# A ring of 7 and 9 staging buffers for the expert weights, in place of 4

## The reference, cut to what matters

```python
def ec_moe(x, w_router, w_gate, w_up, w_down):
    cap = EC_CAPACITY * t // N_EXPERTS
    aff = jax.nn.softmax(jnp.einsum('btd,de->bet', x, w_router), axis=1)
    gate, idx = lax.top_k(aff, cap)
    xs = jax.vmap(lambda xb, ib: xb[ib])(x, idx)
    hid = silu(einsum('becd,edf->becf', xs, w_gate)) * einsum('becd,edf->becf', xs, w_up)
    y = einsum('becf,efd->becd', hid, w_down) * gate[..., None]
    return jax.vmap(lambda yb, ib: jnp.zeros((t, d), yb.dtype).at[ib].add(yb))(y, idx)
```

## Time and profile before

| what | value |
| --- | --- |
| median of three runs | 1483.58 us (1479.49 to 1487.28) |
| the profiled execution: its own time | 1485.16 us |
| its span, first to last instruction | 1483.4 us |
| PE, DVE, ACT, POOL busy | 86%, 60%, 50%, 15% of the span |
| mean rate of all DMA | 218 GB/s (323.19 MB) |
| experts of layer 0, first row transpose to last matmul | 396.9 to 712.6 us |
| experts of layer 1, first row transpose | 1138.65 us |

### The profile page before, as it was taken

One profiled execution on the slowest core, in us unless ns is written; L12 is line 12 of the kernel. 1 busy time (PEld: TensorE's weight loads), 2 busy tenths in 40 slices (PEclk: granted clock), 3 DMA queues, 4 the chain that ended last, 5 costly groups with the idle time before them and its releaser, 6 DMA issues.

```text
span 1483.4 us, 18079 instructions
## 1 busy us (share of the span) xinstructions
PE 1275.2 (86%) x7500; PEld 919.3 (62%) x7500; DVE 886.8 (60%) x997; ACT 736.8 (50%) x866; POOL 218.8 (15%) x128
## 2 busy tenths in 40 slices
PE   5799988997499899999559999999976998999991
PEld 3796856893365555655149994667934655656550
DVE  3613456326688777787164452553257888888883
ACT  3531056415377676776144214453155666666662
POOL 3000000020112121211150000000202023333130
PEclk9897899999699999999779999799997999999996
DMA  9710180004899999999873222002049999999985
GB/s 346 223 61 29 58 298 31 1 29 174 280 324 361 352 355 358 351 366 355 294 211 97 76 61 98 1 1 86 29 170 315 333 351 347 354 347 354 359 311 169
DMA packets 99047, 323.19 MB, mean 218 GB/s; under 512 B 6367, under 2 KB 30142, under 8 KB 82582
## 3 DMA queue, kind: packets, MB, share of 16 engines
q1 hardware_dynamic: 87360, 283.54, 53.3%
q0 software_dynamic: 9152, 30.53, 8.0%
q10 hardware_dynamic: 2454, 7.96, 1.3%
HBM read 298.20 MB, written 23.81 MB: 217 GB/s over the span
## 4 chain that ended last, share of the span: by engine, by line
PE 48%; DMA 21%; ACT 13%; DVE 13%; issue 3%; POOL 1%; ACTq 0%; SPq 0%; POOLq 0%; DVEq 0%
PE psum L821 45%; DVE w_lo L1774 8%; DMA stage<-in_moe_w_up 6%; DMA stage<-in_moe_w_gate 5%; ACT w_hi L1676 5%; DMA stage<-in_moe_w_down 4%; ACT arena L1601 3%; DMA stage<-in_w_mod 2%; DVE arena L2050 2%; DMA h_dram<-arena 1%; DMA acc_dram<-arena 1%; ACT arena L1374 1%; POOL arena L706 1%; DVE h_lo L1774 1%; ACT arena L1423 1%
## 5 line engine op out<-in xcount | busy, mean ns | idle before, releaser
L1774 DVE TENSOR_TENSOR w_lo<-stage,w_hi 128x2048 fp32r<-128x2048 f32 (+1 forms) x216 | 490.7, 2280 | 192.7 <-ACT w_hi L1676 120.7
L1676 ACT ACTIVATE w_hi<-stage 128x2048 fp32r<-128x2048 f32 x192 | 366.6, 1913 | 153.4 <-DMA stage<-in_moe_w_gate 43.0
L821 PE MATMUL psum<-w_hi,h_hi 128*80 128x512 f32 (+1 forms) x848 | 332.4, 392 | 51.8 <-DVE w_lo L1774 40.8
L821 PE MATMUL psum<-w_lo,h_hi 128*80 128x512 f32 (+1 forms) x848 | 326.8, 385 | 0.0
L821 PE MATMUL psum<-w_hi,h_lo 128*80 128x512 f32 (+1 forms) x848 | 326.8, 385 | 0.0
L821 PE MATMUL psum<-h_hi,w_hi 128*128 128x320 f32 x672 | 211.8, 315 | 10.2 <-DVE h_lo L1822 10.2
L821 PEld LDWEIGHTS psum<-w_hi,h_hi 128*80 128x80 f32 (+1 forms) x848 | 130.2, 154 | 132.5 <-DVE w_lo L1774 40.7
L821 PE MATMUL psum<-h_lo,w_hi 128*128 128x320 f32 x672 | 210.3, 313 | 0.0
L821 PE MATMUL psum<-h_hi,w_lo 128*128 128x320 f32 x672 | 210.1, 313 | 0.0
L821 PEld LDWEIGHTS psum<-w_hi,h_lo 128*80 128x80 f32 (+1 forms) x848 | 130.1, 153 | 64.4 <-issue 2.5
L789 POOL DMA_INDIRECT acc_dram<-arena x32 | 94.3, 2946 | 478.7 <-ACT arena L1707 255.0
(11 more groups left out here) (224 smaller groups left out, 1198.5 us busy)
## 6 DMA issues: line engine op xcount, KB each, us to landing
stage<-in_moe_w_gate SPq DMA_DIRECT2D x64, 1024.0 KB, 8.4
stage<-in_moe_w_up SPq DMA_DIRECT2D x64, 1024.0 KB, 8.9
stage<-in_moe_w_down SPq DMA_DIRECT2D x64, 1024.0 KB, 7.3
stage<-in_w_mod SPq DMA_DIRECT2D x48, 1024.0 KB, 7.1
stage<-in_ev_w_in SPq DMA_DIRECT2D x7, 1024.0 KB, 11.8
stage<-in_od_w_in SPq DMA_DIRECT2D x7, 1024.0 KB, 9.9
h_dram<-arena ACTq DMA_DIRECT2D x10, 512.0 KB, 6.7
stage<-in_ev_w_out SPq DMA_DIRECT2D x4, 1024.0 KB, 7.7
```

The lines of the kernel that those rows point to most:

```text
L821: return pe.matmul(o, w, x, start=first, stop=last, skip_group_check=True)
L1676: nc.scalar.activation(split_slot(w_hi, q0), stage[:, PIECE * (p0 % SLOTS):PIECE * (p0 % SLOTS) + PIECE], ACT.Copy)\
L1774: return nc.vector.tensor_tensor(dst, src, hi.bitcast(F32), ALU.subtract)
```

## The change

Five more places of one piece are taken in memory that is free while experts run: place 4 in `arena` at 2048 (where `xs[0]` and `xs[1]` were), 5 and 6 in `arena` at 9248 and 11296, 7 and 8 in `xT` at 1024 and 3072. All four `xs` now lie in `h_hi` and `h_lo`. Layer 0's experts run on a ring of the four staging buffers and 4, 5, 6 (in the order s0, s1, 4, 5, 6, s2, s3); layer 1's on s0 to s3, then 4, 7, 8, 5, 6. All other loads keep the four staging buffers. A piece's place and the piece that had it before stand in the plan (`place`, `earlier`), and each place has a semaphore of its own (`stage_in`, 9 in place of 4).

The first use of a place waits for what lies there: 4, 5 and 6 for the last of the `(L, "h", t)`; 7 and 8 for the last of the `("x out", t)`; in layer 1, 5 and 6 also for all five stores of `x_stored`. The wait for the gather of expert 0 moves from piece 4 to piece 7 (layer 0) and piece 9 (layer 1).

```diff
 SLOTS, SPLITS = 4, 3
+SUM_PLACES, OUT_PLACES, X_PLACES = (4,), (5, 6), (7, 8)
+PLACES = 9
+LENT_PLACES = {0: SUM_PLACES + OUT_PLACES, 1: SUM_PLACES + X_PLACES + OUT_PLACES}
...
+        s = [(staged_count[0] + i) % SLOTS for i in range(SLOTS)]
+        rings[L] = [s[0], s[1], *LENT_PLACES[L], s[2], s[3]] if L == 0 else [*s, *LENT_PLACES[L]]
         for m in range(6 * E):
             q = sum(x["split"] for x in stream)
-            stream.append(dict(key=(L, "moe", m), split=True, used=("moe_used", 6 * E * L + m + 1), p=len(stream), q=q, n=PIECE))
+            stream.append(dict(key=(L, "moe", m), split=True, used=("moe_used", 6 * E * L + m + 1), p=len(stream), q=q, n=PIECE,
+                               place=rings[L][m % len(rings[L])]))
+        staged_count[0] = s[2] if L == 0 else s[0]
+    for x in stream:
+        earlier = [y for y in stream[:x["p"]] if y["place"] == x["place"]]
+        x["earlier"] = earlier[-1] if earlier else None
...
+        def place(n):
+
+            if n < SLOTS:
+                return stage[:, PIECE * n:PIECE * n + PIECE]
+            if n in X_PLACES:
+                at = 1024 + PIECE * X_PLACES.index(n)
+                return xT_[:, at:at + PIECE]
+            at = (2048, 9248, 9248 + PIECE)[(SUM_PLACES + OUT_PLACES).index(n)]
+            return arena[:, at:at + PIECE]
...
-        xs = [arena[0:CAP, 2048 + D * s:2048 + D * s + D] for s in range(2)] + \
-            [h_lo_[0:CAP, 1024 + D * s:1024 + D * s + D].bitcast(F32) for s in range(AHEAD - 2)]
+        xs = [t[0:CAP, 1024 + D * s:1024 + D * s + D].bitcast(F32) for t in (h_hi_, h_lo_) for s in range(2)]
...
-        stage_in = [sem(f"stage_in{s}") for s in range(SLOTS)]
+        stage_in = [sem(f"stage_in{s}") for s in range(PLACES)]
...
                 def expert_piece(e, what):
...
-                    if isinstance(e, int) and m < SLOTS:
-                        before = stream[moe_p[L] + m - SLOTS]
-                        if before["split"]:
-                            sp.wait_ge(lo_ready, before["q"] + 1)
+                    if m < SLOTS + len(lent_places):
+                        if n < SLOTS:
+                            used(sp, pc["earlier"])
+                        elif n in X_PLACES:
+                            filled(sp, ("x out", NT - 1))
                         else:
-                            used(sp, before)
+                            filled(sp, (L, "h", NT - 1))
+                            if L == LAYERS - 1 and n in OUT_PLACES:
+                                sp.wait_ge(x_stored, 16 * NT)
                     else:
-                        if m == SLOTS:
+                        if m == SLOTS + len(lent_places):
                             sp.wait_ge(gathered[0], 16 * (E // AHEAD * L + 1))
-                        sp.wait_ge(lo_ready, m + (moe_q[L] - SLOTS + 1))
+                        sp.wait_ge(lo_ready, pc["earlier"]["q"] + 1)
```

More of the change, by code:

```diff
@@ L286, in plan_weights, with staged @@
 def plan_weights(a):
-    stream = []
+    stream, staged_count, rings = [], [0], {}
+    def staged():
+        staged_count[0] += 1
+        return (staged_count[0] - 1) % SLOTS
     def piece(key, src, split, used):
@@ L296, in piece @@
         q = sum(x["split"] for x in stream)
-        stream.append(dict(key=key, src=src, split=split, used=used, p=len(stream), q=q if split else None, n=n, shape=src.shape[1:]))
+        stream.append(dict(key=key, src=src, split=split, used=used, p=len(stream), q=q if split else None, n=n, shape=src.shape[1:],
+                           place=staged()))
     def rows(w):
@@ L328, in plan_weights @@
             for n in range(2):
-                stream.append(dict(key=(L, "lent", n), split=False, used=(L, "O", PAIRS), p=len(stream), q=None, src=None))
+                stream.append(dict(key=(L, "lent", n), split=False, used=(L, "O", PAIRS), p=len(stream), q=None, src=None, place=staged()))
             out(2), out(3)
         mod((L, "sum")), mod((L, "root")), mod((L, "rank")), mod((L, "top"))
+        s = [(staged_count[0] + i) % SLOTS for i in range(SLOTS)]
+        rings[L] = [s[0], s[1], *LENT_PLACES[L], s[2], s[3]] if L == 0 else [*s, *LENT_PLACES[L]]
         for m in range(6 * E):
             q = sum(x["split"] for x in stream)
-            stream.append(dict(key=(L, "moe", m), split=True, used=("moe_used", 6 * E * L + m + 1), p=len(stream), q=q, n=PIECE))
+            stream.append(dict(key=(L, "moe", m), split=True, used=("moe_used", 6 * E * L + m + 1), p=len(stream), q=q, n=PIECE,
[4 more added lines that the diff above has]
+        x["earlier"] = earlier[-1] if earlier else None
     return stream, {x["key"]: x for x in stream}, {x["q"]: x for x in stream if x["split"]}
@@ L466, in trunk @@
         tmp_o = arena[:, 1280:1280 + NL]
-        lent = [stage[:, PIECE * (piece[(1, "lent", n)]["p"] % SLOTS):][:, 0:PIECE] for n in range(2)]
+        def place(n):
[6 more added lines that the diff above has]
+            return arena[:, at:at + PIECE]
+        lent = [place(piece[(1, "lent", n)]["place"]) for n in range(2)]
         qn = v3(arena, 4480, PAIRS, T)
@@ L586, in slot @@
         def slot(pc):
-            s = PIECE * (pc["p"] % SLOTS)
-            return stage[:, s:s + pc["n"]]
+            return place(pc["place"])[:, 0:pc["n"]]
         def arrived(p):
-            return 16 * sum(x["p"] % SLOTS == p % SLOTS and x["key"][1] != "lent" for x in stream[:p + 1])
+            return 16 * sum(x["place"] == stream[p]["place"] and x["key"][1] != "lent" for x in stream[:p + 1])
         def split_slot(t, q, n=PIECE):
@@ L634, in load @@
                     return
-                if pc["p"] >= SLOTS:
-                    before = stream[pc["p"] - SLOTS]
+                before = pc["earlier"]
+                if before is not None:
                     if before["split"]:
@@ L640, in load @@
                         used(sp, before)
-                sp.dma_start(slot(pc).rearrange("p (k n) -> p k n", k=pc["shape"][0]), pc["src"]).then_inc(stage_in[pc["p"] % SLOTS], 16)
+                sp.dma_start(slot(pc).rearrange("p (k n) -> p k n", k=pc["shape"][0]), pc["src"]).then_inc(stage_in[pc["place"]], 16)
             for L in range(LAYERS):
@@ L652, in expert_piece @@
                 def expert_piece(e, what):
-                    m, m0, half = piece_number(e, what), piece_number(first(e), what), int(what[1])
-                    if isinstance(e, int) and m < SLOTS:
-                        before = stream[moe_p[L] + m - SLOTS]
-                        if before["split"]:
-                            sp.wait_ge(lo_ready, before["q"] + 1)
-                        else:
-                            used(sp, before)
+                    m, half = piece_number(e, what), int(what[1])
+                    pc, lent_places = stream[moe_p[L] + m], LENT_PLACES[L]
+                    n = pc["place"]
+                    if m < SLOTS + len(lent_places):
[3 more added lines that the diff above has]
+                            filled(sp, ("x out", NT - 1))
+                        else:
+                            filled(sp, (L, "h", NT - 1))
+                            if L == LAYERS - 1 and n in OUT_PLACES:
+                                sp.wait_ge(x_stored, 16 * NT)
                     else:
-                        if m == SLOTS:
+                        if m == SLOTS + len(lent_places):
                             sp.wait_ge(gathered[0], 16 * (E // AHEAD * L + 1))
-                        sp.wait_ge(lo_ready, m + (moe_q[L] - SLOTS + 1))
+                        sp.wait_ge(lo_ready, pc["earlier"]["q"] + 1)
                     src = {"g": wg, "u": wu, "d": wd}[what[0]]
-                    ee = slice(e, e + 1) if isinstance(e, int) else bass.ds(lin(e, 1, 0), 1)
                     if what[0] == "d":
-                        src = src[ee, :, 2 * half:2 * half + 2, :]
+                        src = src[e, :, 2 * half:2 * half + 2, :]
                     else:
[L670 to L673, removed]
+                        src = src[e, :, 4 * half:4 * half + 4, :]
+                    sp.dma_start(slot(pc).rearrange("p (k n) -> p k n", k=src.shape[1]), src).then_inc(stage_in[n], 16)
                 for what in ("g0", "g1", "u0", "u1"):
@@ L888, in mod_rows @@
                     w = slot(pc).rearrange("p (k n) -> p k n", k=4)
-                    pe.wait_ge(stage_in[pc["p"] % SLOTS], arrived(pc["p"]))
+                    pe.wait_ge(stage_in[pc["place"]], arrived(pc["p"]))
                     for k in range(4):
@@ L1378, in split @@
                 pc = piece[key]
-                act.wait_ge(stage_in[pc["p"] % SLOTS], arrived(pc["p"]))
+                act.wait_ge(stage_in[pc["place"]], arrived(pc["p"]))
                 if pc["q"] >= SPLITS:
@@ L1571, in _ @@
                     for n in range(2):
-                        used(act, stream[piece[(1, "lent", n)]["p"] - SLOTS])
+                        used(act, piece[(1, "lent", n)]["earlier"])
```

(7 more changed lines are left out.)

## The result

The changed kernel takes 1439.05 us (median; 1438.07 to 1442.09) against 1485.18 us: a ratio of 0.9706, interval 0.9685 to 0.9728. That is 46 us, where 10 were predicted.

What follows compares the result with a forecast made beforehand. The prediction took the experts to follow a DMA already full in the long stretches. Gains of 2.4 (layer 0), 3.5 (layer 1) and 3.8 us (long stretches) sum to 9.7 us, giving 1474 us; range 1466 to 1484.

Steps and rivals of the forecast that it cites:

- the load takes 10 us because it queues behind others, and a longer queue moves no more bytes: Expert stretches, 444 to 700 and 1186 to 1440 us: DMA shares 1.01 and 1.00 mean full engines, so experts follow the DMA.
- the long stretches: Full expert windows of both layers: small gaps where all four buffers wait should go, 3.8 us gained, bounds 0 and 7.7.
- More buffers can only win DMA time that is idle now: Around the experts' starts in both layers: gain limited to idle DMA, 12.1 us in all beside small gaps.
- The head start: Before the experts: three more early pieces in layer 0 (7.7 us, net 2.4), five in layer 1 (3.5 us).
- The delay of the stores: Layer 0, `h_dram` stores beside early loads: last landing at 395 us, 5.3 us late, PE starting near 402.2.
- the 0.23 window: Layer 0, 388 to 396 us, 6.2 us of idle DMA: moves to some 396 to 402 us, about 2 us shorter.
- the 0.69 window: Layer 1, 1134 to 1138 us, 1.2 us of idle DMA: its share becomes 1.0.
- Layer 1's start: First row transpose waits for ACT, not the gather; gather 1 to 3 us longer, taken as 1.5, counted at nothing.
- Landing of expert loads gets longer: Sign to look for in expert loads: each takes longer to land than now; no size given.
- with no more GB/s: Expert loads: the longer landing comes without a higher DMA rate.
- full pay: Rival: stores keep their pace, each of eight extra pieces saves 2.57 us, 20.6 us in all, 1463 us; chance 0.17.
- the slower rival: First gathers take 9.8 us beside loads in both layers, experts start 14.5 us later in all, 1498 us; chance 0.08.

Runs made afterwards that it cites:

- once: Changed kernel, but the extra places are filled only once ahead of the experts, then the ring has four staging buffers; 1485.29 us, ratio 1.0014 to the kernel before.

## Why the prediction was wrong

The direction was right, the size and the cause were not, and the time lies outside the range.

- The step that failed is the first: "the load takes 10 us because it queues behind others, and a longer queue moves no more bytes". It was read from shares of 1.01 and 1.00. The share adds up the packets' times, and these held time in which little moved: away from gathers and scatters the loads moved 379 GB/s with 2.5 of them under way and 415 with 4.5, both at a share near 1. The rows to compare were the rates: 357 and 353 GB/s in the long stretches, 408 in the row for loads alone. The round of 14.3 us in the earlier trace rows was set aside as appearance; four pieces in 14.3 us are 293 GB/s, where PE takes 358, and the runs with more places show that the number of places was the limit.
- So the term "the long stretches", 3.8 us with bounds of 0 and 7.7 us, is the one that was mis-sized: 42.6 us of the span came out of the experts' stretches. The number that it should have been held against was in the text, PE's waits of 21.6 + 17.7 = 39.3 us; in the stretches that answer to them (445 to 685 and 1166 to 1420 us) 1.6 and 0.2 us are left. "More buffers can only win DMA time that is idle now" put it aside.
- The head start, 7.7 us of DMA work in layer 0 and 3.5 us of filled gaps in layer 1, brought nothing alone (`once`: 1.0014). The prediction saw that PE sets the pace from 412 to 436 us, and did not draw from it that early pieces are lost there with a ring of four. With the deep ring, leaving the head start out cost nothing either (1438.55 us).
- The delay of the stores has the right mechanism, and 3.4 us in place of 5.3. PE's start moved by 1.4 us, since the gather landed after 4.13 us in place of 6.16: the shorter gather was not foreseen. Layer 0's pieces were issued about as forecast (5.8 us after the first load; 375.7 - 369.25 = 6.5 forecast), and the 0.23 window became 0.90, the 0.69 window before layer 1's experts 1.02.
- Layer 1's start was taken to have slack: a gather 1 to 3 us longer, at no cost, and by an estimate 3.2 us for its bytes beside two other queues (a duration, which was held against a delay of 1 to 3 us). It landed after 8.84 us in place of 4.17, and PE waits for it; from 1110 to 1119 us the gathers moved 0.45 of 3.65 MB, an eighth in place of the quarter of that estimate. Two of the five extra pieces were not ahead at all: the last store to `acc_dram` landed after 15.1 us (before, 3.5 to 3.9), and they were issued at 1124.1 and 1124.5 us, 5 us after PE's start.
- "Landing of expert loads gets longer" came true (8.6 us before, 13.6 in the changed kernel, mean of the loads issued from 445 to 650 us); "with no more GB/s" did not.
- The rivals: full pay came nearest in size, but its mechanism (each extra piece in memory saves its DMA time) is the one that `once` excludes. Of the slower rival, the longer first gather came in layer 1 (8.84 us) and not in layer 0 (4.13), and it was made up for many times over.

What stays open: what a load packet waits for when few loads are under way, and on which engines. The rate goes with the number of loads under way; why it does, the traces don't tell, as they have queues and not single engines.

## What to carry to other kernels

A DMA share of 1.00 does not say that the engines can move no more: compare the GB/s with a stretch where the same loads run alone, and if the rate is lower while a consumer waits, look at the ring's round trip. Size a ring for the other traffic beside it: here four places were enough for the loads alone and not beside the gathers and scatters, and one more gave two thirds of the gain. The runs take away the bytes of that traffic together with its bursts, so they don't tell which of the two counts. A head start is not worth much by itself: with a ring of four it was gone by 445 us, and with the deep ring it could be left out.

## What the runs showed of the hardware

Away from gathers and scatters, loads of 1 MB moved 415 GB/s in the changed kernel, with 4.5 loads under way on average, and 379 GB/s in the kernel before, with 2.5, at shares of 1.02 and 1.00 (445 to 650 us). Beside a gather and a scatter the loads got 1.01 MB of 1.55 MB in 5 us, 59.1% of the engines' time by this count.
